# The normed activations moved 32 bytes along each partition

## The reference

```
proj = rmsnorm(h, norm_mix_g) @ w_in + b_in            # 2048 -> 11272
merged = sigmoid(gm) * (hm @ w_branch_m) + sigmoid(gc) * (yc @ w_branch_c)
h = h + merged @ w_out
u = causal_dwconv(rmsnorm(h, norm_ffn_g) @ w_up, ...)  # 2048 -> 11008
h = h + (silu(gate) * val) @ w_down                    # 5504 -> 2048
proj = rms_norm(x, g_pre0) @ l0_gla_w_in               # 2048 -> 6160
proj = rms_norm(x, g_pre1) @ l1_mla_w_in               # 2048 -> 3136
```

## The kernel before

| tensor | first byte | modulo 128 | modulo 256 |
|---|---|---|---|
| w_hi | 49,280 | 0 | 128 |
| w_lo | 65,664 | 0 | 128 |
| n_hi | 82,048 | 0 | 128 |
| n_lo | 98,432 | 0 | 128 |
| arena start (yc_hi, f_hi, og_hi, mo_hi) | 129,600 | 64 | 64 |

## Time and profile before

### The profile page before, as it was taken

How to read it: one execution, slowest core, us unless ns; L and a number is a source line. 1 busy time by engine, 2 the same in 40 slices (tenths; PEclk the granted TensorE clock), 3 DMA queues, 4 the chain that set the end, 5 groups by cost and what they waited for, 6 DMA issues and landing times.

```text
span 2255.0 us, 46586 instructions
## 1 busy us (share of the span) xinstructions
PE 2177.2 (97%) x17596; PEld 2134.9 (95%) x17596; DVE 1302.1 (58%) x1641; ACT 1188.7 (53%) x1565; POOL 255.6 (11%) x325
## 2 busy tenths in 40 slices
PE   6999999999999999999999999999999979999996
PEld 5999999999999999999999999999998969999996
DVE  5555654444456666666665555556665465756544
ACT  5444445545446656666665454644554444555542
POOL 2000000000110000000001111000100123111111
PEclk7999999999999999999999999999999999999998
DMA  3445445555555544545546555445444433444453
GB/s 148 170 171 181 167 167 187 186 186 186 182 191 187 186 178 175 186 168 185 186 170 218 208 209 219 169 170 185 169 166 170 177 138 132 169 149 149 149 183 114
DMA packets 54927, 393.83 MB, mean 175 GB/s; under 512 B 6097, under 2 KB 6225, under 8 KB 7522
## 3 DMA queue, kind: packets, MB, share of 16 engines
q1 hardware_dynamic: 54432, 392.19, 48.6%
q10 hardware_dynamic: 450, 1.02, 0.1%
HBM read 391.09 MB, written 2.10 MB: 174 GB/s over the span
## 4 chain that ended last, share of the span: by engine, by line
PE 62%; issue 18%; DVE 9%; ACT 6%; POOL 3%; DVEq 1%; ACTq 1%; DMA 0%; POOLq 0%
PE acc L552 18%; PE acc L554 17%; PE acc L553 17%; ACT w_hi L919 4%; DVE w_lo L1324 3%; PE tok L594 2%; PE tok L595 2%; PE tok L596 2%; DVE f_pre L1549 1%; ACT L1095 1%; DVE f_val L1560 1%; DVE f_val L1556 1%; DVE f_act L1569 1%; POOL sumsq_g L1892 1%; PE att L612 1%
## 5 line engine op out<-in xcount | busy, mean ns | idle before, releaser
L1324 DVE TENSOR_TENSOR w_lo<-raw,w_hi 128x1024 fp32r<-128x1024 f32 x740 | 904.9, 1236 | 802.7 <-ACT w_hi L919 801.0
L552 PE MATMUL acc<-n_hi,w_hi 128*128 128x256 f32 x3488 | 999.9, 287 | 26.6 <-POOL n_lo L1901 19.0
L554 PE MATMUL acc<-n_hi,w_lo 128*128 128x256 f32 x3488 | 991.6, 284 | 0.0
L553 PE MATMUL acc<-n_lo,w_hi 128*128 128x256 f32 x3488 | 991.5, 284 | 0.0
L919 ACT ACTIVATE w_hi<-raw 128x1024 fp32r<-128x1024 f32 x740 | 760.2, 1052 | 385.3 <-PE acc L554 167.8
L552 PEld LDWEIGHTS acc<-n_hi,w_hi 128*128 128x128 f32 x3488 | 673.9, 193 | 32.5 <-issue 23.4
L553 PEld LDWEIGHTS acc<-n_lo,w_hi 128*128 128x128 f32 x3488 | 674.2, 193 | 0.5
L554 PEld LDWEIGHTS acc<-n_hi,w_lo 128*128 128x128 f32 x3488 | 674.1, 193 | 0.0
L552 PE MATMUL acc<-f_hi,w_hi 128*128 128x256 f32 x688 | 189.9, 276 | 0.0
L553 PE MATMUL acc<-f_lo,w_hi 128*128 128x256 f32 x688 | 189.9, 276 | 0.0
L554 PE MATMUL acc<-f_hi,w_lo 128*128 128x256 f32 x688 | 189.9, 276 | 0.0
(11 more groups left out here) (313 smaller groups left out, 2980.6 us busy)
## 6 DMA issues: line engine op xcount, KB each, us to landing
raw<-stream_in SPq DMA_DIRECT2D x370, 1024.0 KB, 4.8
x<-x_in SPq DMA_DIRECT2D x4, 512.0 KB, 7.3
out<-x SPq DMA_DIRECT2D x4, 512.0 KB, 2.7
v_bias<-v_bias_in ACTq DMA_DIRECT2D x1, 512.0 KB, 8.8
par<-params_in ACTq DMA_DIRECT2D x1, 287.0 KB, 5.3
pos_i<-positions_in ACTq DMA_DIRECT2D x1, 128.0 KB, 6.7
gk<-gk_in ACTq DMA_DIRECT2D x1, 68.0 KB
```

Of the source, the lines that this page charges most:

```text
L552: nc.tensor.matmul(out, w_hi[:, s, wc], hi[:, k, :], start=first, stop=False)
L553: nc.tensor.matmul(out, w_hi[:, s, wc], lo[:, k, :], start=False, stop=False)
L554: return nc.tensor.matmul(out, w_lo[:, s, wc], hi[:, k, :], start=False, stop=last)
L1324: nc.vector.tensor_tensor(w_lo[:, s, :], raw[:, s, :], w_hi[:, s, :].bitcast(fp32), ALU.subtract).then_inc(lo_ready, 1)
```

## The change

Eight floats (32 bytes) named `apart` are declared between `w_lo` and `n_hi`, and nothing reads or writes them. All tensors from `n_hi` to `eps_eps_col` start 32 bytes later: `n_hi` at 82,080 and `n_lo` at 98,464, which is 32 modulo 128 and 160 modulo 256. The rule for the arena's start is rewritten; it gives 129,600 as before, so nothing in the arena moves, and `x`, `raw`, `w_hi`, `w_lo` stay too. No instruction is added, removed or moved on any engine.

```
+LINE = 128
...
         w_lo = sb("w_lo", [P, RING, UNIT], fp32r)
+        apart = sb("apart", [P, 8])
         n_hi = sb("n_hi", [P, KT, T], fp32r)
         n_lo = sb("n_lo", [P, KT, T], fp32r)
...
-        arena_start = -(-nc.sbuf_base // 64) * 64
+        arena_start = -(-(nc.sbuf_base - LINE // 2) // LINE) * LINE + LINE // 2
         arena_end = nc.sbuf_usable_end
```

## The result

The changed kernel takes 2239.32 us (median of 4 runs, 2238.66 to 2241.93) against 2256.49 us (4 runs, 2254.41 to 2258.77) for the one before: a ratio of 0.9919, 95% interval 0.9907 to 0.9931. (The ratios of this document are the recorded estimates; they differ from the ratio of the two medians, here 0.9924, by up to 0.002.) It is faster by 17 us, where 57 had been forecast.

The account below looks back on a forecast made before the run. It took the matmul stream's pace on PE to bound the kernel. Terms of -37.8, -21.3 and +2.5 us gave -56.6 on 2256.7, so 2200.1, median 2202 us; 8-in-10 range 2182 to 2296.

Parts of the forecast that it names:

- The cause, n_*'s place against the weights: Feature-tile matmuls: n_* starts at the weights' place modulo 128, so the two streams collide, costing 6.7 ns in 120.
- Does anything else become late?: wup at 113.3 ns, some 472 us: ACT and DVE would be 65% and 69% busy, DMA 191 GB/s, so no loss.
- issue: Whole-span chain of waits: an 18% share beside PE's 62%, read as stretches where PE itself streams.
- The pace term: Feature tiles with n_*, 10,464 matmuls: from 120.0 ns to the arena's paces, 113.3 or 117.8; merge and wup 37.8 us less.
- The restarted stages: Gates, mix, rank, gla, latent, krope, mla, 4800 matmuls: between 10.6 and 32.0 us less, the middle 21.3 taken.
- all at 117.8: Case where every feature tile takes the arena's slower pace: -23.0 + 2.5 us, kernel at 2238 us.
- Token tiles: n_* as stationary operand: 384 matmuls 512 wide charged 2.5 us more; 256 wide between -2.6 and +2.6, taken as 0.
- Other moved tensors at 0: Norms: normed, square, parameters and ones, used by ACT, DVE and POOL; a tenth would be 3.5 us, taken as 0.
- Nothing changes: Rival: 32 bytes are not seen or place was never the cause; n_* stays at 120, 2258.5 us; chance 0.12.
- The signed distance: Rival: moving place minus weight place modulo 256 sets the pace; feature tiles go to 123.3 ns, 2291 us; chance 0.27.
- Half a step: Rival: tiles beginning inside a 64-byte piece read one piece more, 6.67 ns per matmul, 2333 us; chance 0.11.
- Better than the arena: Rival: 32 is the middle of the good places, paces of 110 ns or less, below 2182 us; chance 0.05.

Follow-up runs that it names:

- e1: Kernel before, with n_hi and n_lo left in place and only the other tensors that the change moved shifted 32 bytes: 2258.60 us, ratio 0.9997.
- e10: Kernel before, with the 32 empty bytes ahead of w_hi, so weights and n_* move together at distance 0, the arena left in place: 2275.87 us (one run).
- e2: Kernel before, with ScalarE's loop over wup written 7 x 6 feature tiles instead of 21 x 2: 2253.26 us, ratio 0.9983.
- e3: Changed kernel, with ScalarE's loop over wup written 7 x 6 feature tiles instead of 21 x 2: 2225.69 us, ratio 0.9855.
- e7: Kernel before, with n_* begun 192 bytes past the weights' place modulo 256, the arena's own place: 2235.08 us, ratio 0.9902.
- e4: Kernel before, with n_* begun 64 bytes past the weights' place, g_both declared ahead of n_hi: 2252.48 us, ratio 0.9957.
- e8: Kernel before, with n_* at 192 as in e7 and ScalarE's loop over wup written 7 x 6: 2226.36 us, ratio 0.9859.
- e12: e8 with the matmul of the feed-forward norm's sum issued three times: 2224.44 us, ratio 0.9862.

## Why the prediction was right in direction and wrong in size

- **The cause, n_*'s place against the weights: right.** The kernel is faster, the gain is gone with n_* back at 0 (e1), and at distance 0 the 120.0 ns come back wherever the pair stands (e10). The Trainium skill, "TensorE: Matmul & The Clock Gate", Part 2, "Step-by-step", has two independent read ports, so that a weight load takes no read bandwidth from the running matmul. If nothing else tied the two reads, the distance between the operands should not matter; by distance alone the pace was 120.0, 117 or 113.3 ns, at a granted clock of 1.00 in wup. What the two reads share is not shown.
- **The failed step: "Does anything else become late?", with its answer "So the cover holds".** wup was to give 4128 x 6.67 = 27.5 us and gave 0.4. I compared ACT's and DVE's busy shares, 65% and 69%, with the room they had. But their work in wup is a cycle: convolution taps, f_act, f_hi, a table load, the copy of the weights, w_lo, f_pre, f_gate, a second table load, Silu, and again. The cycle takes 23.4 us a pass at every pace tried, 0.34 to 0.36 more than the 192 matmuls at 120.0 ns. It has no room to be faster, however idle each engine is. Had I asked for the chain of the stretch, and not of the whole span, I would have seen PE at 17% of it. My own last sentence, a wait of PE on the line of w_lo, names half of what came: the weight loads waited 14.1 us for it, and PE 10.7 for f_pre. e2 and e3 show it: with the cycle shortened, wup gives 13.0 us more with the change. That makes 13.4 of the 27.5; the rest is the pace, 117.8 in e3 and not 113.3. In e7, with many pieces at 113.4, the cycle still held wup at 499.2.
- **"issue" misread.** I put the 18% of the earlier trace rows to PE streaming. In wup it is, in the piece shown, the tail of a table load on ACT.
- **The pace term mis-sized: 113.3 taken, 116.7 to 117.8 measured.** I took the arena's paces for a place that no row showed. Merge was to give 10.2 us and gave 4.5; 1536 matmuls x 3.1 ns = 4.8. The restarted stages were to give 21.3, and 18.8 with the charge for the token tiles that lie in them: mix gave 5.4, gla 1.7 and mla 2.7, together 9.8. In this the "all at 117.8" of the prediction, 2238 us, lies by chance on the result: its -23.0 us hold 9.1 for wup (4128 x 2.2), which did not come, while the matmuls elsewhere got 2.6 to 3.1 ns and mlaout gave 3.4 us that nobody had counted.
- **Token tiles: right for 512 wide** (233.3, so 384 x 6.6 = 2.5 us more, which is why gla gives only 1.7). 256 wide went from 119.9 to 118.4, 0.6 us less, taken as 0. The charge had luck in it: the token tiles of c_*, from which it was read the earlier trace rows, have two paces themselves, without being moved: before, one of the four ran at 228.8 ns and three at 233.4; after, all four at 228.8.
- **Other moved tensors at 0: right** (e1, for all but two small ones).
- **Not foreseen: -3.4 us in mlaout,** from a tensor that was not moved. mo_* ran at 117.8 before and at 113.3 after: its stream ran on the other pace. The earlier trace rows showed both paces at the same distance, and I put that to how the stream begins, but counted only n_* for it. That the paces can flip in an untouched stage, by 3.4 us in mlaout and 9.2 in wdown, follows from e4, e8 and e12.
- **The rivals.** Nothing changes: false. The signed distance: false, 32 gives less than 120 and 96 gives as much. Half a step: false. Better than the arena: false at 32.

Left open: why the pace at 96 is that of 0 and at 128 between, and which of its paces a stream takes. A place of 224 was not tried.

## What to carry to other kernels

Before a stage is called bound by an engine, take the chain of waits of that stage alone: two engines at 62% and 65% that wait for each other in a cycle hold the time as firmly as one at 100%, and the cycle's period (here 23.38 us against 23.04 of matmuls) can be read from one line's starts. Place moving operands and weights by trying it: with 128 x 256 fp32r matmuls that load new weights every time, the distance modulo 256 decided between 113 and 120 ns a matmul, and most places gave more than one pace, so a single profiled run doesn't tell what a place is worth. And where a loop body on ScalarE needs two activation tables, try a longer body: here that was worth 4 us by itself and 13.6 more on top of the change.

## What the runs showed of the hardware

- The pace of back-to-back matmuls depends on the moving operand's bytes against the weights', modulo 256: 120.0 ns at 0 and 96; 116.7 or 117.8 at 32; 113.3 or 117.8 at 64 and 192; 118.65 or 120.0 at 128; 117.3, 118.65 or 120.0 at 160. The granted clock was 1.00 in merge, wup and wdown of all these runs.
- At every other place tried than 0 and 96 the same matmuls ran at two or three paces. At 192 the pace changed only at restarts and was kept for 6191 matmuls in e8, from n_* to f_*; at 32 it also changed without a wait (117.8 to 116.7). So an untouched stage can change by 4%: wdown 233.8 or 243.0 us.
- An activation table load took 1.28 us and came twice in each pass of the loop body. The Trainium skill, "ScalarE activation tables: per-element evaluation and per-set limits", "Table sets in the compiler and the runtime", says that loads are placed per block; the trace agrees, 42 loads in 21 passes and 14 in 7. Behind the load the next instruction began at once (858.01 + 1.28, 859.30).
